# Expert weights in plain fp32 column tiles from a ring of nine buffers, one 2 MB transfer for each matrix

## What is computed

```python
def expert_block(args):
    xb, e = args
    hid = jax.nn.silu(xb @ w_gate[e]) * (xb @ w_up[e])
    return hid @ w_down[e]
```

## Time and profile before

| | |
|---|---|
| timed runs | 1157.61, 1158.18, 1159.35 us (median 1158.18) |
| profiled execution, first to last instruction (its span) | 1156.5 us |
| PE busy with matmuls | 1124.8 us, 97% |
| DVE, ACT busy | 827.9 us, 643.6 us |
| expert loop on PE | about 550 to 1123.65 us |
| DMA, busy share of the 16 engines from 580 to 1080 us | 1.01 |

### The profile page before, as it was taken

How to read it: one execution, slowest core, us unless ns; L and a number is a source line. 1 busy time by engine, 2 the same in 40 slices (tenths; PEclk the granted TensorE clock), 3 DMA queues, 4 the chain that set the end, 5 groups by cost and what they waited for, 6 DMA issues and landing times.

```text
span 1156.5 us, 17522 instructions
## 1 busy us (share of the span) xinstructions
PE 1124.8 (97%) x7034; PEld 884.0 (76%) x7034; DVE 827.9 (72%) x1181; ACT 643.6 (56%) x796; POOL 110.7 (10%) x131
## 2 busy tenths in 40 slices
PE   7999999999999999999899999999999999999995
PEld 6999999999957768887577777777777777777762
DVE  5414435223377658888988898898898888988886
ACT  7221241211068733334687777777777777778844
POOL 1002110012000000000031000111100111012110
PEclk9999999999999999999999999999999999999999
DMA  7216474433050051115899999999999999999867
GB/s 240 73 38 189 130 247 138 144 98 122 2 180 24 26 222 74 74 73 209 329 403 405 381 394 387 386 398 379 384 390 380 381 393 385 387 385 373 330 263 299
DMA packets 77941, 292.49 MB, mean 253 GB/s; under 512 B 9702, under 2 KB 34406, under 8 KB 52962
## 3 DMA queue, kind: packets, MB, share of 16 engines
q1 hardware_dynamic: 65010, 255.55, 58.4%
q0 software_dynamic: 11680, 31.57, 8.3%
q10 hardware_dynamic: 1168, 4.23, 0.9%
HBM read 270.09 MB, written 33.77 MB: 263 GB/s over the span
## 4 chain that ended last, share of the span: by engine, by line
PE 92%; DVE 4%; ACT 1%; DMA 1%; issue 1%; SPq 0%; ACTq 0%; DVEq 0%; POOLq 0%
PE psum L1224 10%; PE psum L1223 10%; PE psum L1222 10%; PE psum L859 8%; PE psum L861 8%; PE psum L860 8%; PE psum L1251 5%; PE psum L1253 5%; PE psum L1252 5%; PE psum L994 3%; PE psum L996 2%; PE psum L995 2%; PE psum L1211 2%; PE psum L944 2%; PE psum L960 1%; PE psum L938 1%
## 5 line engine op out<-in xcount | busy, mean ns | idle before, releaser
L859 PE MATMUL psum<-h_hi,w_hi 128*128 128x344 f32 (+2 forms) x576 | 185.8, 323 | 3.0 <-DVE h_lo L1738 2.9
L861 PE MATMUL psum<-h_hi,w_lo 128*128 128x344 f32 (+2 forms) x576 | 184.0, 319 | 0.0
L860 PE MATMUL psum<-h_lo,w_hi 128*128 128x344 f32 (+2 forms) x576 | 183.9, 319 | 0.0
L2194 DVE TENSOR_TENSOR w_down_lo<-w_down,w_down_hi 128x2048 fp32r<-128x2048 f32 x62 | 139.7, 2289 | 41.9 <-ACT w_down_hi L1549 41.6
L2194 DVE TENSOR_TENSOR w_gate_lo<-w_gate,w_gate_hi 128x2048 fp32r<-128x2048 f32 x64 | 144.3, 2289 | 17.7 <-ACT w_gate_hi L1549 17.6
L2194 DVE TENSOR_TENSOR w_up_lo<-w_up,w_up_hi 128x2048 fp32r<-128x2048 f32 x64 | 143.7, 2286 | 2.1
L1549 ACT CAST w_gate_hi<-w_gate 128x2048 fp32r<-128x2048 f32 x64 | 120.0, 1920 | 9.4 <-DMA w_gate<-in_w_gate 9.2
L1549 ACT CAST w_up_hi<-w_up 128x2048 fp32r<-128x2048 f32 x64 | 120.4, 1926 | 3.4 <-DMA w_up<-in_w_up 3.2
L1549 ACT CAST w_down_hi<-w_down 128x2048 fp32r<-128x2048 f32 x62 | 115.8, 1911 | 2.4 <-DMA w_down<-in_w_down 2.4
L859 PEld LDWEIGHTS psum<-h_hi,w_hi 128*128 128x128 f32 x576 | 108.2, 188 | 5.5 <-DVE h_lo L1738 3.8
L861 PEld LDWEIGHTS psum<-h_hi,w_lo 128*128 128x128 f32 x576 | 108.2, 188 | 0.0
(11 more groups left out here) (310 smaller groups left out, 1925.1 us busy)
## 6 DMA issues: line engine op xcount, KB each, us to landing
w_gate<-in_w_gate SPq DMA_DIRECT2D x64, 1024.0 KB, 17.3
w_up<-in_w_up SPq DMA_DIRECT2D x64, 1024.0 KB, 17.2
w_down<-in_w_down SPq DMA_DIRECT2D x64, 1024.0 KB, 15.4
w_raw<-in_w_in SPq DMA_DIRECT2D x24, 512.0 KB, 4.4
y_tile<-y_rows SPq DMA_DIRECT2D x16, 512.0 KB, 10.9
kv<-in_cache_k POOLq DMA_DIRECT2D x24, 256.0 KB, 4.5
kv<-in_cache_v POOLq DMA_DIRECT2D x24, 256.0 KB, 4.5
x_tile<-in_x_prompt SPq DMA_DIRECT2D x8, 512.0 KB, 5.2
```

The lines of the kernel that those rows point to most:

```text
L859: mm(ps, wh[:, k, :], h_hi[:, k, cols], start=(k == 0), stop=False)
L860: mm(ps, wh[:, k, :], h_lo[:, k, cols], start=False, stop=False)
L861: ins = mm(ps, wl[:, k, :], h_hi[:, k, cols], start=False, stop=(k == KD - 1))
L2194: vec.tensor_tensor(dst[:, part, :], src[:, part, :], hi[:, part, :].bitcast(F32), ALU.subtract).then_inc(split, 1)
```

## The change

Expert weights are no longer split: matrices are used as they land, in plain fp32. The 96 rows of an expert are cut into 64 (`HEAD`) and 32 (`TAIL`). For the 64, two matmuls with 64 stationary columns write the two halves of the partitions of a PSUM bank: up and gate in `head_gate_up` (L numbers are those of the diff), the two halves of the output in `head_down`. For the 32, four matmuls with 32 stationary columns and 256 moving columns write the four quarters (`tail_gate_up`, `tail_down`). All nine units form a ring (`RING`) that is filled in the order of `items`; each matrix is one transfer of 2 MB. A unit is loaded again when `tail_done` (gate, up) or `y_done` (down) of its user has come. The layout of `wo_hi` and `wo_lo` is by half, so that two of their units are free earlier, and five matrices are issued before the output projection ends. ACT and DVE share the copies of the results. `store_h2` and `store_residual` move from SP's queue to POOL's. The tiles of the final stage move to other units.

```diff
+HEAD = 64
+TAIL = SLOTS - HEAD
+QUART = 256
...
-        wo_hi = at("wo_hi", WOUT, [KD, D], F32R)
-        wo_lo = at("wo_lo", WOUT + 32768, [KD, D], F32R)
+        wo_hi = at("wo_hi", WOUT, [2, KD, 512], F32R)
+        wo_lo = at("wo_lo", WOUT + 32768, [2, KD, 512], F32R)
...
-        wg = [at(f"w_gate{s}", unit(u), [KD, DE]) for s, u in enumerate((0, 3))]
...
-        wg_hi = at("w_gate_hi", unit(2), [KD, DE], F32R)
...
+        RING = (0, 6, 7, 2, 4, 1, 3, 5, 8)
+        ring = [at(f"expert_w{i}", unit(u), [2 * HALF]) for i, u in enumerate(RING)]
...
+        xg_first = at("x_rows_first", MISC, [D])[0:SLOTS]
...
+        hid = pack("hid", [DE])
...
+        items = [("gate", 0), ("up", 0)]
+        for e in range(1, NE):
+            items += [("gate", e), ("up", e), ("down", e - 1)]
+        items += [("down", NE - 1)]
...
-            def load_gate(f, s, e, halves=(0, 1)):
...
+            def load_weights(i):
+                kind, e = items[i]
+                sp.dma_start(ring[i % len(RING)], a[f"w_{kind}"][order[e] * P:(order[e] + 1) * P, :]
+                             ).then_inc(landed[i % len(RING)], 16)
             sp.wait_ge(attended, NSTEP)
...
+            load_weights(0)
+            sp.wait_ge(a_ready, NT - 1)
+            load_weights(1)
+            load_weights(2)
+            sp.wait_ge(o_ready, 4 * NT - 2)
+            load_weights(3)
+            load_weights(4)
             sp.wait_ge(o_ready, 4 * NT)
...
+            for i in (5, 6, 7):
+                load_weights(i)
             sp.wait_ge(first.xT_ready, 2)
...
+            sp.wait_ge(gates_ready, 1)
+            sp.wait_ge(h2_out[0], 16 * 5)
+            load_weights(8)
+            for i in range(len(RING), len(items)):
+                kind, e = items[i - len(RING)]
+                if kind == "down":
+                    sp.wait_ge(first.y_done, e + 1)
+                else:
+                    sp.wait_ge(first.tail_done, e + 1)
+                load_weights(i)
...
+            def head_gate_up(f, n, gate, gate_in, up, up_in, uses):
+                if not isinstance(n, int) or n > 0:
+                    pe.wait_ge(f.head_hid, n)
+                pe.wait_ge(gate_in, uses[0])
+                pe.wait_ge(up_in, uses[1])
                 for k in range(KD):
                     if k % 4 == 0:
...
-                    mm(bank(b)[0:SLOTS, :], xT_hi[:, k, :], hi[:, k, :], start=(k == 0), stop=False)
-                    mm(bank(b)[0:SLOTS, :], xT_hi[:, k, :], lo[:, k, :], start=False, stop=False)
-                    ins = mm(bank(b)[0:SLOTS, :], xT_lo[:, k, :], hi[:, k, :], start=False, stop=(k == KD - 1))
...
+                        pe.wait_ge(f.xT_done, 2 * n + (k // 4 + 1))
+                    mm(bank(0)[0:HEAD, :], xT[:, k, 0:HEAD], up[:, k, :], start=(k == 0), stop=(k == KD - 1),
...
+                    ins = mm(bank(0)[HEAD:P, :], xT[:, k, 0:HEAD], gate[:, k, :], start=(k == 0), stop=(k == KD - 1),
...
+                ins.then_inc(f.head_done, 1)
+            def tail_gate_up(f, n, gate, up):
+                if not isinstance(n, int) or n > 0:
+                    pe.wait_ge(f.tail_hid, n)
+                for k in range(KD):
+                    for g, (w, q) in enumerate(((gate, 0), (gate, 1), (up, 0), (up, 1))):
+                        ins = mm(bank(1)[TAIL * g:TAIL * (g + 1), 0:QUART], xT[:, k, HEAD:SLOTS],
+                                 w[:, k, q * QUART:(q + 1) * QUART], start=(k == 0), stop=(k == KD - 1),
...
+                ins.then_inc(f.tail_done, 1)
...
             def turn_hidden(f, n):
...
+                if isinstance(n, int) and n == 0:
+                    pe.wait_ge(hid_cleared, 1)
+                pe.wait_ge(f.head_hid, n + 1)
+                pe.wait_ge(f.tail_hid, n + 1)
                 for m in range(DE // P):
...
+                    ins = nc.tensor.transpose(bank(6)[:, m * P:(m + 1) * P], hid[:, m * P:(m + 1) * P], ident)
                 ins.then_inc(f.hT_ready, 1)
...
+            def tail_down(f, n, w, w_in, uses, hT):
+                pe.wait_ge(f.hT_done, n + 1)
+                if not isinstance(n, int) or n > 0:
+                    pe.wait_ge(f.tail_out, 2 * n)
+                pe.wait_ge(w_in, uses)
                 for m in range(DE // P):
...
+                    for q in range(4):
+                        ins = mm(bank(3)[TAIL * q:TAIL * (q + 1), 0:QUART], tail_of(hT, m),
+                                 w[:, m, q * QUART:(q + 1) * QUART], start=(m == 0), stop=(m == DE // P - 1),
...
+                ins.then_inc(f.tail_y_done, 1)
...
+            def head_down(f, n, w, hT):
+                if not isinstance(n, int) or n > 0:
+                    pe.wait_ge(f.y_out, 2 * n)
+                for m in range(DE // P):
                     for half in range(2):
...
-                        mm(out, hT_hi[:, m, :], wd_hi[:, m, cols], start=(m == 0), stop=False)
...
-                        ins = mm(out, hT_lo[:, m, :], wd_hi[:, m, cols], start=False, stop=(m == DE // P - 1))
+                        ins = mm(bank(2)[HEAD * half:HEAD * (half + 1), :], hT[:, m, 0:HEAD],
+                                 w[:, m, half * 512:(half + 1) * 512], start=(m == 0), stop=(m == DE // P - 1),
...
                 ins.then_inc(f.y_done, 1)
...
+            gate_up(0)
+            for b in range(NE):
+                if b >= 1:
+                    tail_down(first, b - 1, weights_of("down", b - 1), *landing_of("down", b - 1), hT[(b - 1) % 2])
+                turn_hidden(first, b)
                 if b + 1 < NE:
                     pe.wait_ge(first.rows_in, 16 * (b + 2))
                     turn_rows(first)
                 if b >= 1:
...
+                    head_down(first, b - 1, weights_of("down", b - 1), hT[(b - 1) % 2])
+                if b + 1 < NE:
+                    gate_up(b + 1)
+            tail_down(first, NE - 1, weights_of("down", NE - 1), *landing_of("down", NE - 1), hT[(NE - 1) % 2])
+            head_down(first, NE - 1, weights_of("down", NE - 1), hT[(NE - 1) % 2])
             keep_clock(6, bank(0), 512)
...
+            def silu_head(f, n):
+                act.wait_ge(f.head_done, n + 1)
                 if not isinstance(n, int) or n > 0:
...
+                    act.wait_ge(f.head_hid, n)
+                nc.scalar.activation(sg[0:HEAD, :], bank(0)[HEAD:P, :], ACT.Silu).then_inc(f.head_silu, 1)
+            def silu_tail(f, n):
+                act.wait_ge(f.tail_done, n + 1)
+                if not isinstance(n, int) or n > 0:
+                    act.wait_ge(f.tail_hid, n)
+                nc.scalar.activation(sg[HEAD:P, 0:QUART], bank(1)[0:HEAD, 0:QUART], ACT.Silu).then_inc(f.tail_silu, 1)
+            def copy_tail_y(f, n, ysb=ysb):
+                act.wait_ge(f.tail_y_done, n + 1)
+                for q in range(2):
+                    ins = nc.scalar.copy(ysb[HEAD:SLOTS, q * QUART:(q + 1) * QUART],
+                                         bank(3)[TAIL * q:TAIL * (q + 1), 0:QUART])
+                ins.then_inc(f.tail_out, 1)
+            def copy_head_y(f, n, ysb=ysb):
                 act.wait_ge(f.y_done, n + 1)
...
+                nc.scalar.copy(ysb[0:HEAD, 0:512], bank(2)[0:HEAD, :]).then_inc(f.y_out, 1)
...
+            act.wait_ge(out_misc, 16 * 4)
+            for b in range(NE):
+                silu_head(first, b)
+                silu_tail(first, b)
+                into = y_second_last if b == NE - 1 else ysb
+                if b >= 1:
+                    if b >= 2 and b < NE - 1:
+                        act.wait_ge(first.sent, 16 * (b - 1))
+                    copy_tail_y(first, b - 1, into)
                 if b + 1 < NE:
...
+                    copy_rows(first, b + 1)
                 if b >= 1:
...
+            def hidden_head(f, n):
+                dve.wait_ge(f.head_silu, n + 1)
+                if not isinstance(n, int) or n > 0:
+                    dve.wait_ge(f.hT_ready, n)
+                vec.tensor_tensor(hid[0:HEAD, :], bank(0)[0:HEAD, :], sg[0:HEAD, :], ALU.mult).then_inc(f.head_hid, 1)
+            def hidden_tail(f, n):
+                dve.wait_ge(f.tail_silu, n + 1)
+                vec.tensor_tensor(hid[HEAD:P, 0:QUART], bank(1)[HEAD:P, 0:QUART], sg[HEAD:P, 0:QUART], ALU.mult
+                                  ).then_inc(f.tail_hid, 1)
+            def copy_hidden(f, n, hT):
+                dve.wait_ge(f.hT_ready, n + 1)
+                vec.tensor_copy(hT, bank(6).rearrange("p (m t) -> p m t", m=DE // P)).then_inc(f.hT_done, 1)
+            def copy_tail_y(f, n, ysb=ysb):
+                dve.wait_ge(f.tail_y_done, n + 1)
+                for q in range(2, 4):
+                    ins = vec.tensor_copy(ysb[HEAD:SLOTS, q * QUART:(q + 1) * QUART],
+                                          bank(3)[TAIL * q:TAIL * (q + 1), 0:QUART])
+                ins.then_inc(f.tail_out, 1)
+            def copy_head_y(f, n, ysb=ysb):
+                dve.wait_ge(f.y_done, n + 1)
```

(35 more changed lines are left out.)

381 lines of the change are left out of this document (105 added, 276 removed).

## The result

| | kernel before | kernel after |
|---|---|---|
| median of the runs | 1158.3 us | 1147.53 us (1145.50 to 1149.07) |
| profiled execution | span 1156.5 us | span 1143.7 us |
| predicted | | 1128 us (1117 to 1146) |

The ratio is 0.9903, with a 95% interval of 0.9889 to 0.9917: faster by 1%, little more than a third of what was forecast, and above the range. On the spans the gain is 12.8 us where 30.4 were predicted, so 17.6 us are missing. The profiled execution of after was the fastest of its four, so on the medians 19.5 us are missing; what follows accounts for the 17.6.

What follows compares the result with a forecast made beforehand. PE and DMA were both full, with PE pacing: loop end 1092.2 + 1.0 - 1123.65 = -30.4 us on the 1156.5 span gives 1126.1; the median, 1.7 above, is 1128 us, range 1117 to 1146.

Steps and rivals of the forecast that it cites:

- The lead holds to the end, by 6 us: Weight loads in the expert loop: expert 31's pair lands at 1064 us, PE wants it at 1070.7.
- Matmuls, shapes, transposes: PE's period per expert in the loop: 15.48 + 0.33 + 0.61 + 0.5 = 16.9 us, with column groups overlapping fully.
- Slower: Rival: column groups in head and tail overlap only in part; at factor 1.6 period 20.6 us, about 1245 us; chance 0.08.
- One transfer for two: Expert matrix loads: one transfer in place of two changes only the wait's grain, priced at 0 us.
- From 574 on the engines work without a pause: DMA loads after expert 1's gate and up: continuous, with up of expert 5 landing at about 603.7 us.
- D: The DMA engines' own period per expert in the loop, put at 17.6 to 17.85 us and counted as 17.7.
- The moved stores: Stores moved to POOL's queue: last `h2` store delays the gather of expert 1; charged 1 us, between nothing and 4.
- A new wait each period: Rival: PE waits before `turn_hidden`, or ACT is late with rows after a slow scatter; 1134 to 1154 us; chance 0.17.
- The end: Last matmul to scattered rows' first add: halved copies save 0.35 us, DVE's queued adds cost as much; 0 net.
- DMA takes over, a slower D: Rival: the loads' slower period sets the loop's end; 1134 to 1150 us, 1141 at D = 18.5; chance 0.06.

Runs made afterwards that it cites:

- gather_clear: Kernel after, but weight loads of items 3 to 7 issued only when the first expert's gathered rows are in; 1151.46 us.
- count_two: Kernel after with two 1 MB transfers per expert matrix and TensorE's token count moved before the first expert's matmuls; 1143.87 us, ratio 0.9875.
- two_halves: Kernel after with each expert matrix loaded by two transfers of 1 MB (8 KB packets) instead of one of 2 MB; 1141.89 us, ratio 0.9849.
- marker_two: Kernel after with two 1 MB transfers per matrix and VectorE's last five first-choice additions waiting until POOL has issued the last scatter; 1145.96 us, one execution.
- halves_start: Kernel after with two 1 MB transfers per matrix for items 0 to 8 only, 2 MB from item 9 on; 1146.96 us.
- after_again: Kernel after, unchanged, run again beside two 1 MB transfers per matrix on one chip; 1148.57 us.

## Why the prediction was wrong

*The step that failed: "The lead holds to the end, by 6 us".* PE alone would have ended at 1139.6 on after's own start; what ended last was the load of `up` of expert 31, which came at 1084.1 us, 20 us after my 1064. Three runs part the 17.6 us that are missing from the predicted span of 1126.1. With halves and without the gathers' bytes, where PE paces to the end, the span is 1133.0 (one execution): 6.9 us are PE's period and the end. With halves and the gathers it is 1139.1: 6.1 us are a stream that binds even with transfers of 1 MB. In after it is 1143.7: 4.6 us are the transfers of 2 MB.

*Matmuls, shapes, transposes: right.* 17.02 us a period against 16.9, full overlap in head and tail. The 0.12 make 3.6 us over 30 periods. (In the rival "Slower" I spread a factor for pairs over the whole 15.36 us. On the 10.3 us of the pairs alone it gives 18.1 instead of 19.2, and a time near 1210 instead of 1245. It was not needed.)

*One transfer for two, "I take 0": wrong.* It is worth 5.6 and 6.3 us on the medians of two pairs, 5.7 on the kernel before. I had asked what the size does to the wait's grain and not what it does to others: a gather or scatter lands after 7.2 to 7.7, 8.2 to 8.7 or 10.3 to 11.5 us beside packets of 4, 8 or 16 KB. The Trainium skill, "DMA: Bandwidth & Descriptors", section "Queues, rings and completion order", has each engine change between queues only after a whole packet; the three latencies agree with that in kind, if a packet of the profile is one of the page's, which nothing here tells. At the start this delays the first gather, PE pauses longer, and the clock falls. I had kept 549.96 for head of expert 0; it was 555.8.

*"From 574 on the engines work without a pause": the pause came before it.* Items 8 to 10 could only be issued at 564.6 to 567.2, when the queue had run dry (DMA share 0.61 and 0.76 in the ten us before and after 560). `up` of expert 5 was in at 613.8, not 603.7. And the period was 18.09 from there, not 17.7: 10 us more over 26 experts. With the 10 us of the later start these are the 20 us. I had put D between the queue's bytes, 17.6, and 17.85 from the growth of the landings, and counted with 17.7. The bytes still say 17.6 in after, where landings say 18.06: the count is a mean, and a matrix is in when its last part is.

*The moved stores, 1 us:* the gather of expert 1 was issued at 557.46, not 551.53, behind the last `h2` store. It was in the end hidden (no wait of PE for it in after), and it decided in `gather_clear` and `count_two`. No run shows the 1 us that I charged.

*The rival "A new wait each period": its condition came, its cost did not.* I had written "3 us more and ACT is late, and only some 6 us more PE". Scatters did land about 3 us later, and ACT waits for them in nearly every period (waits of ACT, 600 to 900 us: us, times, longest), yet PE has no idle time there:

```profile
ACT y_rows L1542 <- DMA y_rows<-y_rows,sidx: 38.3, 16, 3.4
```

*The end, "0": wrong.* From the loop's last matmul to the end of the span are 37.3 us (1106.35 to 1143.7) where 32.9 were before, 4.5 us more; with 0.2 in the last tiles and less the 1 us charged for the stores this is, within rounding, the 3.8 of the sum below. On the chain of after the last scatter lands 7.54 us after its issue begins, before 3.94: these 3.6 us are its stretched issue (4.72 us; before 1.15). Another 0.8 is VectorE's: its additions end at 1106.56, after the last matmul, and three copies follow. But 3.6 is not what a short issue gives back: in `two_halves` the chain runs over the additions and TensorE's residual matmuls instead, and `marker_two` was no faster. The queued additions that I priced by their own time cost by what they held up.

The 17.6 missing us, along after's own path: start 6.1 (580.09 against 574.0), pace 3.6, end 3.8: PE alone would have ended at 580.09 + 559.5 = 1139.6. The stream adds 4.1. But these do not simply add. `halves_start` gives back most of the first and gains nothing, since the stream is then the later of the two. The rival "DMA takes over, a slower D" is the one that came true, at D = 18.06; I had priced it for 18.5 and given it 0.06. Its formula with 18.06 and my start of 603.7 ends the loop at 1095, only 3 us late; it took the start of 613.8 as well.

*Left open:* why some of the sixteen parts of the loads fall behind. Halves and the gathers' bytes both bear on it, but no run parts their shares, and the steps are not told apart by engine. In each run a few experts' matrices land 19 to 21 us after those of the one before (expert 13 in all six kernels of the table with whole loads and all gathers). That the clock fell because of the longer pause is argued from its coming right behind it in some kernels and not in others; no run changed the pause alone. Nor was a ring of more than nine places tried, as there is no room for it.

## What to carry to other kernels

When two resources are both full before a change, price the change by two finishing times, one for each, and carry the start of each separately: the later one is the answer, and repairing the other gives nothing. Take a stream's period from landings of one matrix to the same matrix of the next expert, not from bytes per time: the bytes are a mean over parts that can drift apart, here by 28 us. Choose the size of a big transfer also by what small, urgent transfers must wait behind: here 8 KB a partition beat both 4 and 16, and `two_halves` (1141.9 us) beats both kernels of this study.

## What the runs showed of the hardware

- The granted clock fell to 0.50 behind an idle time of PE of 2.72 us in after (for 10 us) and of 1.85 us in `after_again` (for 17 us), both after gathers of 10.2 to 11.1 us; behind 0.96 us in `two_halves` it stayed at 1.00, as it did from 540 to 560 in every kernel with halves at the start and TensorE's work whole. 1.00 is the level of 2.4 GHz, 0.50 that of 1.2. The fall itself cost more than the wait: the head of expert 0 starts 6.6 us later in after than in `two_halves` (555.73 and 549.12), of which the gather is 1.75.
- Issuing an indirect DMA on POOL takes 0.9 to 1.0 us in the loop, and 3.5 to 4.7 us beside VectorE's additions of two SBUF inputs.
- Packets of 4, 8 and 16 KB: 381, 388 and 389 GB/s in all (one profiled execution each).
- The sixteen parts of a load stream drift apart when it is full: within 1.4 us of each other at expert 3 and 28.4 us at expert 31 in after, 3.4 and 10.0 in `two_halves`.
